# Two-layer decoder trunk, expert stage: slots in tiles of 64 and 32 instead of tiles of 32, down products of 512 columns

## The reference, cut to what matters

```python
D_MODEL = 1024; SEQ = 256; N_EXPERTS = 8; TOP_K = 2; D_FF_EXPERT = 3584
...
logits = (ht @ w_router).astype(jnp.float32) + b_router.astype(jnp.float32)
top_val, top_idx = lax.top_k(logits, TOP_K)
gates = jax.nn.softmax(top_val, axis=-1)
combine = jnp.sum(jax.nn.one_hot(top_idx, N_EXPERTS, dtype=jnp.float32) * gates[..., None], axis=1)
y = jnp.zeros_like(ht)
for e in range(N_EXPERTS):
    y = y + combine[:, e:e + 1].astype(h.dtype) * swiglu(ht, w_gate[e], w_up[e], w_down[e])
```

## Time and profile before

| | us |
|---|---|
| median of 3 runs | 1287.14 (1286.01 to 1287.77) |
| the profiled execution's own time | 1287.23 |
| its span, first to last instruction | 1285.4 |
| first product of the expert stage | at 464.13 |
| pairs 1, 2, 3 begin | at 663.80, 861.77, 1068.67 |
| last product of the small down of pair 3 ends | at 1274.93 |

### The profile page before, as it was taken

How to read it: one execution, slowest core, us unless ns; L and a number is a source line. 1 busy time by engine, 2 the same in 40 slices (tenths; PEclk the granted TensorE clock), 3 DMA queues, 4 the chain that set the end, 5 groups by cost and what they waited for, 6 DMA issues and landing times.

```text
span 1285.4 us, 27220 instructions
## 1 busy us (share of the span) xinstructions
PE 1233.9 (96%) x12500; PEld 712.8 (55%) x12501; DVE 338.3 (26%) x701; ACT 285.9 (22%) x499; POOL 39.3 (3%) x48
## 2 busy tenths in 40 slices
PE   7988999999999999999999999999997999998896
PEld 6865788888856763334653344653342664333364
DVE  5787565445357440000010010010020000001001
ACT  5575563434248411010000010000000000000000
POOL 1012000000003100000000000000000000000000
PEclk9999999999998999999999999999999999999999
DMA  9642455464453589999999999999999999999994
GB/s 352 233 131 97 134 177 185 129 236 160 113 178 132 222 369 412 412 415 425 424 424 425 427 425 425 424 424 426 425 427 426 425 424 424 425 427 426 425 423 170
DMA packets 64108, 423.64 MB, mean 330 GB/s; under 512 B 5760, under 2 KB 13686, under 8 KB 39414
## 3 DMA queue, kind: packets, MB, share of 16 engines
q1 hardware_dynamic: 62780, 419.09, 80.9%
q0 software_dynamic: 992, 2.69, 0.7%
q10 hardware_dynamic: 218, 0.08, 0.0%
HBM read 420.77 MB, written 1.07 MB: 328 GB/s over the span
## 4 chain that ended last, share of the span: by engine, by line
PE 81%; DMA 10%; DVE 4%; ACT 3%; issue 1%; SPq 0%; DVEq 0%; ACTq 0%
PE PS L2311 33%; PE PS L2340 16%; PE PS L1733 7%; PE PS L1737 7%; PE PS L1734 7%; DMA places_raw<-in_w_down_o_dram 6%; DMA places<-in_w_down_o_dram 3%; PE PS L2076 2%; PE PS L2348 2%; PE PS L2250 1%; DVE w_r L947 1%; PE PS L2233 1%; ACT w_r L487 1%; PE PS L2088 1%; DMA raw<-in_w_in_e_dram 0%
## 5 line engine op out<-in xcount | busy, mean ns | idle before, releaser
L2311 PE MATMUL PS<-places_raw,xe 128*32 128x512 f32 (+1 forms) x3760 | 362.4, 540 | 10.8 <-DMA places_raw<-in_w_up_o_dram 10.8
L2311 PEld LDWEIGHTS PS<-places_raw,xe 128*32 128x32 f32 x3760 | 119.4, 110 | 240.8 <-issue 218.8
L1733 PE MATMUL PS<-w_r,a_hi 128*128 128x512 f32 (+4 forms) x400 | 148.1, 374 | 3.5 <-DVE a_lo L976 2.5
L1734 PE MATMUL PS<-w_r,a_lo 128*128 128x512 f32 (+4 forms) x400 | 145.5, 367 | 0.0
L947 DVE TENSOR_TENSOR w_r<-raw,w_r 128x2048 fp32r<-128x2048 f32 (+4 forms) x61 | 128.9, 2142 | 42.0 <-ACT w_r L487 41.8
L2311 PE MATMUL PS<-places,xe 128*32 128x512 f32 (+1 forms) x1360 | 133.3, 540 | 4.1 <-DMA places<-in_w_up_o_dram 4.1
L487 ACT ACTIVATE w_r<-raw 128x2048 fp32r<-128x2048 f32 (+4 forms) x61 | 106.4, 1800 | 15.0 <-PE PS L1737 13.1
L2340 PE MATMUL PS<-places_raw,e_l 128*32 128x256 f32 x1848 | 106.4, 380 | 2.1 <-DMA places_raw<-in_w_down_o_dram 2.1
L1737 PE MATMUL PS<-w_r,a_hi 128*128 128x512 f32 (+4 forms) x400 | 103.7, 367 | 0.3 <-DVE w_r L947 0.3
L2311 PEld LDWEIGHTS PS<-places,xe 128*32 128x32 f32 x1360 | 43.3, 110 | 87.8 <-issue 80.2
L1733 PEld LDWEIGHTS PS<-w_r,a_hi 128*128 128x128 f32 x400 | 76.3, 191 | 17.4 <-issue 5.1
(11 more groups left out here) (328 smaller groups left out, 1011.6 us busy)
## 6 DMA issues: line engine op xcount, KB each, us to landing
places_raw<-in_w_gate_o_dram SPq DMA_DIRECT2D x48, 1792.0 KB, 27.0
places_raw<-in_w_up_o_dram SPq DMA_DIRECT2D x46, 1792.0 KB, 31.6
places_raw<-in_w_down_o_dram SPq DMA_DIRECT2D x44, 1792.0 KB, 37.2
places<-in_w_down_o_dram SPq DMA_DIRECT2D x19, 1792.0 KB, 36.5
places<-in_w_up_o_dram SPq DMA_DIRECT2D x18, 1792.0 KB, 32.5
places<-in_w_gate_o_dram SPq DMA_DIRECT2D x16, 1792.0 KB, 30.7
raw<-in_w_in_e_dram SPq DMA_DIRECT2D x12, 1024.0 KB, 9.8
raw<-in_w_down_e_dram SPq DMA_DIRECT2D x11, 1024.0 KB, 5.1
```

The lines of the kernel that those rows point to most:

```text
L1733: nc.tensor.matmul(dst, xh, wh, start=first, stop=False)
L1734: nc.tensor.matmul(dst, xl, wh, start=False, stop=False)
L2311: ins = nc.tensor.matmul(PS[g * Q:(g + 1) * Q, bank + c0 // NT, 0:c], xe[:, at, x0:x0 + Q], w[:, g * QW + c0:g * QW + c0 + c], start=at == ...
```

## The change

Tiles of the gate and up products: the first 64 slots are one block, loaded into two groups of 64 array columns. Pass `j` = 0 streams weight quarters 0 and 2, pass `j` = 1 quarters 1 and 3. The last 32 slots of a large expert stay a tile of 32 on four groups. Down: per block `kk` two matmuls of 512 columns for the 64 slots (each on one group of 64), and for a large expert four of 256 columns on groups of 32 as before. The results and the way back follow: `y_l` is [64 slots in two halves of the outputs] plus the tail's quarters, `y_s` one tile of 512 columns copied by ACT alone (DVE's `small_result` is gone), three pick matrices a pair instead of five, and `bring_back` contracts over 64 rows and, for the tail, over 32. Quarters are brought back and added in the order 0, 2, 1, 3.

```diff
+HALF_TILE = P // 2
+L_BLOCKS, BLOCKS = 2, 3
+BACK_ORDER = (0, 2, 1, 3)
...
-        LARGE_GATE, LARGE_UP, LARGE_DOWN = (2, 4, 0), (6, 2, 4), (0, 1, 6)
-        SMALL_GATE, SMALL_UP, SMALL_DOWN = (0, 6), (2, 4), (7, 5)
+        LARGE_GATE, LARGE_UP, LARGE_DOWN = (2, 4, 0), (6, 2, 4), (0, 1)
+        SMALL_GATE, SMALL_UP, SMALL_DOWN = (0, 6), (2, 4), 7
...
-        PICKS = ((2, 0), (2, S), (3, 0), (4, 0), (4, S))
+        PICKS = ((2, 0), (2, S), (4, 0))
...
-                for j in range(L_TILES):
-                    nc.scalar.activation(y_l[:, j, :], PS[:, LARGE_DOWN[j], 0:YC], ACT.Copy).then_inc(sem("l_y"), 1)
+                nc.scalar.activation(y_l[:, 0:NT], PS[:, LARGE_DOWN[0], :], ACT.Copy).then_inc(sem("l_y"), 1)
+                nc.scalar.activation(y_l[:, NT:NT + YC], PS[:, LARGE_DOWN[1], 0:YC], ACT.Copy).then_inc(sem("l_y"), 1)
...
-                nc.scalar.activation(y_s[:, 0, :], PS[:, SMALL_DOWN[0], 0:YC], ACT.Copy).then_inc(sem("s_y0"), 1)
+                nc.scalar.activation(y_s[:, :], PS[:, SMALL_DOWN, :], ACT.Copy).then_inc(sem("s_y"), 1)
...
             def return_picks(p):
 
+                if p:
+                    dve.wait_ge(mm_done, C_MOE + p * PAIR_CHUNKS)
...
-            def small_result(p):
-                dve.wait_ge(mm_done, C_MOE + (p + 1) * PAIR_CHUNKS)
-                nc.vector.tensor_copy(y_s[:, 1, :], PS[:, SMALL_DOWN[1], 0:YC]).then_inc(sem("s_y1"), 1)
...
-            def bring_back(of, y, tiles, banks):
+            def bring_back(of, y, tail_of, tail_y, banks):
 
                 for t in range(TT):
-                    for j in range(tiles):
-                        for g in range(4):
-                            rows_g = slice(g * Q, (g + 1) * Q)
-                            ins = nc.tensor.matmul(PS[:, banks[g], t * YC:(t + 1) * YC], of[rows_g, j, t * P:(t + 1) * P],
-                                                   y[rows_g, j, :], start=j == 0, stop=j == tiles - 1)
-                            if t == TT - 1 and j == tiles - 1:
-                                ins.then_inc(sem("moe_sc"), 1)
+                    rows_t, out = slice(t * P, (t + 1) * P), slice(t * YC, (t + 1) * YC)
+                    for g in BACK_ORDER:
+                        rows_c = slice(g // 2 * HALF_TILE, (g // 2 + 1) * HALF_TILE)
+                        ins = nc.tensor.matmul(PS[:, banks[g], out], of[rows_c, rows_t], y[rows_c, g % 2 * YC:(g % 2 + 1) * YC],
+                                               start=True, stop=tail_y is None)
+                        if tail_y is None and t == TT - 1:
+                            ins.then_inc(sem("moe_sc"), 1)
+                    for g in BACK_ORDER if tail_y is not None else ():
+                        rows_g = slice(g * Q, (g + 1) * Q)
+                        ins = nc.tensor.matmul(PS[:, banks[g], out], tail_of[rows_g, rows_t], tail_y[rows_g, :],
+                                               start=False, stop=True)
+                        if t == TT - 1:
+                            ins.then_inc(sem("moe_sc"), 1)
...
-                x0 = (L_CAP if small else 0) + j * Q
                 bank = {"g": (LARGE_GATE, SMALL_GATE), "u": (LARGE_UP, SMALL_UP)}[kind][small][j]
+                if j < 2:
+                    x0, n, of = (L_CAP if small else 0), HALF_TILE, lambda g: (2 * g + j) * QW
+                else:
+                    x0, n, of = HALF_TILE, Q, lambda g: g * QW
                 for c0, c in ((0, NT), (NT, QW - NT)):
-                    for g in range(4):
-                        ins = nc.tensor.matmul(PS[g * Q:(g + 1) * Q, bank + c0 // NT, 0:c], xe[:, at, x0:x0 + Q],
-                                               w[:, g * QW + c0:g * QW + c0 + c], start=at == 0, stop=at == DC - 1)
+                    for g in range(P // n):
+                        ins = nc.tensor.matmul(PS[g * n:(g + 1) * n, bank + c0 // NT, 0:c], xe[:, at, x0:x0 + n],
+                                               w[:, of(g) + c0:of(g) + c0 + c], start=at == 0, stop=at == DC - 1)
...
-                    for j in range(S_TILES if small else L_TILES):
-                        bank = (SMALL_DOWN if small else LARGE_DOWN)[j]
+                    first, last = G == 0 and kk == 0, G == 3 and kk == QB - 1
+                    at = kk * P + G // 2 * HALF_TILE
+                    for c in range(2):
+                        ins = nc.tensor.matmul(PS[c * HALF_TILE:(c + 1) * HALF_TILE, SMALL_DOWN if small else LARGE_DOWN[0], :],
+                                               acts[:, G % 2, at:at + HALF_TILE], down_columns(n - half, kk, c * NT, NT),
+                                               start=first, stop=last)
+                    if not small:
+                        at = kk * P + G * Q
                         for g in range(4):
-                            ins = nc.tensor.matmul(PS[g * Q:(g + 1) * Q, bank, 0:YC],
-                                                   acts[:, j, kk * P + G * Q:kk * P + (G + 1) * Q], down_columns(n - half, kk, g),
-                                                   start=G == 0 and kk == 0, stop=G == 3 and kk == QB - 1)
+                            ins = nc.tensor.matmul(PS[g * Q:(g + 1) * Q, LARGE_DOWN[1], 0:YC], acts[:, 2, at:at + Q],
+                                                   down_columns(n - half, kk, g * YC, YC), start=first, stop=last)
```

More of the change, by code:

```diff
@@ L225, in hybrid_trunk @@
         e_l, z = place(z0, "e_l", [P, L_TILES, QW])
[L226 removed]
+        y_l, _ = place(z0, "y_l", [P, NT + YC])
         rt, _ = place(z0, "rt", [P, 9, TT * NE * NE])
[L228 to L229 removed]
+        y_s, _ = place(z, "y_s", [P, NT])
+        gpick, _ = place(z + NT, "gpick", [P, TT, BLOCKS, P])
         e_s, z = place(z, "e_s", [P, S_TILES, QW])
[L231 removed]
+        back_s, z = place(z, "back_s", [P, S])
+        z += S
         places, z2 = place(z, "places", [P, 3, EW])
@@ L464, in _ @@
                 sp.wait_ge(sem("spare_add"), 4 * SPARES)
-            for g in range(4):
+            for n, g in enumerate(BACK_ORDER):
                 cols = slice(g * YC, (g + 1) * YC)
-                sp.wait_ge(sem("moe_add"), 8 * PAIRS - 3 + g)
+                sp.wait_ge(sem("moe_add"), 8 * PAIRS - 3 + n)
                 sp.dma_start(out[0].rearrange("(t p) d -> p t d", p=P)[:, :, cols], X[:, :, cols]).then_inc(sem("stored"), 16)
@@ L1544, in return_picks @@
             def return_picks(p):
+                if p:
+                    dve.wait_ge(mm_done, C_MOE + p * PAIR_CHUNKS)
                 for t in range(TT):
[L1547 to L1550, removed]
+                    for j, (e, s0, n) in enumerate(((p, 0, HALF_TILE), (p, HALF_TILE, Q), (p + PAIRS, 0, HALF_TILE))):
+                        ins = nc.vector.tensor_scalar(gpick[:, t, j, :].rearrange("p (a s) -> p a s", s=n),
+                                                      iota[:, s0:s0 + n].unsqueeze(1).to_broadcast([P, P // n, n]),
                                                       pos[:, t, e:e + 1], comb[:, t, e:e + 1], ALU.is_equal, ALU.mult)
@@ L1608, in pair @@
                     gathered(p + 1)
-                for g in range(4):
+                for g in BACK_ORDER:
                     add_back(2 * p, g, BACK_L[g])
-                small_result(p)
                 if not follow:
-                    for g in range(4):
+                    for g in BACK_ORDER:
                         add_back(2 * p + 1, g, LAST_BACK[g])
@@ L2242, in turn_picks @@
                 ins.then_inc(sem("moe_turn"), 1)
[L2244 removed]
+            def bring_back(of, y, tail_of, tail_y, banks):
                 for t in range(TT):
[L2247 to L2253 removed]
+                    rows_t, out = slice(t * P, (t + 1) * P), slice(t * YC, (t + 1) * YC)
+                    for g in BACK_ORDER:
+                        rows_c = slice(g // 2 * HALF_TILE, (g // 2 + 1) * HALF_TILE)
[9 more added lines that the diff above has]
+                            ins.then_inc(sem("moe_sc"), 1)
             def back_large(p):
[L2257 to L2258 removed]
+                pe.wait_ge(sem("l_y"), L_BLOCKS * (p + 1))
+                bring_back(back_l[:, 0, :], y_l[:, 0:NT], back_l[:, 1, :], y_l[:, NT:NT + YC], BACK_L)
             def back_small(p, banks):
[L2262 to L2264 removed]
+                pe.wait_ge(sem("s_y"), p + 1)
+                bring_back(back_s, y_s, None, None, banks)
             def two_rows(block, f):
@@ L2277, in tile_waits @@
                 elif k == 0 and j == 1:
-                    if p:
-                        pe.wait_ge(sem("s_y1"), p)
-                    else:
+                    if not p:
                         pe.wait_ge(sem("x_dve"), 1)
@@ L2319, in gate_up, with down_columns @@
                 ins.then_inc(mm_done, 1)
-            def down_columns(n, kk, g):
-                if kk < 3 or (kk == 3 and g < 2):
-                    return place_of(n)[:, kk * D + g * YC:kk * D + (g + 1) * YC]
-                return place_of(n + 1)[:, kk * D + g * YC - EW:kk * D + (g + 1) * YC - EW]
```

(4 more changed lines are left out.)

14 lines of the change are left out of this document (6 added, 8 removed).

## The result

| | before | changed |
|---|---|---|
| median us | 1286.88 (1286.01 to 1287.77, 4 runs) | 1312.48 (1312.23 to 1315.52, 4 runs) |
| ratio | 1 | 1.0205, 95% interval 1.0188 to 1.0221 |
| profiled execution: own time, span | 1287.23, 1285.4 | 1315.52, 1313.7 |
| expert stage, first product to last | 464.13 to 1274.93, 810.8 | 465.98 to 1303.27, 837.3 |

The changed kernel is 2% slower, 25.6 us in the medians. The forecast was 1313.5. One of the ten executions of the first grouped kernel further down ran at a granted clock of 0.75 and took 1601.42 us, and its ratio leaves it out.

A forecast was written before the change was run, and what follows sets the result against it. The transfers bound the kernel, PE having 21.7 us in hand. PE's end, 1253.2 + 47.4 + 0.7 = 1301.3, passes the transfers' 1274.9; with the tail's -0.2 that is +26.2, so 1313.5 us, range 1300 to 1322.

The forecast's parts named there:

- The bound: Expert stage: the transfers bound the old kernel, and PE has 21.7 us in hand.
- Streamed columns, side by side: Large gate, up and down products: no streaming saved, two 64-wide groups run side by side, 0.435 us for two rounds.
- Rival D: Gate, up and down: groups of 64 don't overlap for 512 columns, some 1840 us; chance 1%.
- Fewer instructions: nothing: PE's matmuls: no overhead in an instruction that a wider one could save, so no gain.
- Rival E: Whole kernel: it gets faster; only the tail's -0.2 us is left, PE can't pull the transfers; chance 2%.
- Changes of width: Large-expert chunks: 340 changes between 64 and 32 columns, 0.16 or 0.12 us each, add 47.4 us on PE.
- small terms: PE: way back +1.7 us, 64-wide after 128-wide work +0.9, fewer pick transposes -1.9; sum +0.7.
- The tail: After the last product: single ACT copy +0.2 us, earlier adds on DVE -0.4, together -0.2.
- The slack as a rule: PE in the expert stage: added work is free up to 21.7 us and counts in full beyond.
- Rival A: Expert stage: the change of width costs nothing or under 0.06 us, transfers still bound, 1287 us; chance 11%.
- B: Width changes: only the leaving costs, 0.10 us each, 1300 us, the low end; with forecast and C 86%.
- C: Each width change costs half a way to 128 and back, 1322 us, the high end; with forecast and B 86%.

The follow-up runs named there:

- grouped kernel: The changed kernel with 64-wide and 32-wide products reordered to stand together, 96 changes of width instead of 340: 1284.27 us, repeated with more rounds 1282.78 us.
- half loads: From the twelfth chunk on only half of each chunk is loaded, PE's work unchanged: kernel before 1266.98 us, changed kernel 1313.84 us.
- kernels with 18 us more: The kernel before with 18.1 us of 32-wide tile passes repeated: over all four pairs 1294.59 us, in pairs 2 and 3 alone 1290.39 us.
- split one: The grouped kernel with every gate and up matmul of 512 or 384 columns split into two of half the columns: 1287.26 us, ratio 1.0001.

## Why the prediction was right

*The bound.* Right. PE had some 21 us to wait out in the old kernel (half loads: 21.1 below the kernel before of the same runs, worked out 21.7), none in the new one.

*Streamed columns, side by side.* Right: a 64-wide round of 512 takes 0.43 us for both groups; the rounds start 0.43 us apart, 0.48 right after a change of width. Rival D is gone.

*Fewer instructions: nothing.* Right for PE's time and wrong for the kernel as a whole. The step costed only what an instruction costs on TensorE. What the number of instructions does to the transfers, by their fetches as it seems, was left out, and where the transfers are the bound it is worth some 4 us. In the changed kernel, which PE bounds, it is hidden. Rival E rested on the same gap: "PE can't pull the transfers" is so, but with fewer instructions the last weights land earlier, and the grouped kernel is 0.2 to 0.3% faster than the one before.

*Changes of width.* The step that carries the sum. 340 changes at 0.12 and 0.16 gave 47.4 us; with the small terms 48.1 for the stage's four pairs, 12.0 each. Pair 1 grew by 12.03. The stage grew by 26.5 us (worked out 26.4). So the number came out right because its parts did, each within 1 us, and not by luck: the slack was 21.1 us by the half loads (worked out 21.7), and the added work 46.9 (worked out 47.9). That neighbours' prices can be composed, the leaving by one and the first load by the other, held to 0.01 us. The 64-wide half of a block holds its first load and the leaving of 64, 0.05 + 0.10 by the prediction's prices and 1.01 - 0.86 = 0.15 in the chain; the 32-wide half 0.02 + 0.11, and 0.57 - 0.435 = 0.135 in the chain. The rule of the Trainium skill (TensorEngine Tiling (Array Packing), Key Properties), that a change of tiling mode drains TensorE, agrees with this trace for 64 against 32, where the way there and back costs 0.28 us; the page has no figure.

*The tail.* -0.2 worked out, -0.26 measured.

*Against the median.* The profiled execution of the changed kernel lies 3.0 us above the median of its four. Its stage begins 1.85 us later than in the kernel before, in code that was not changed: over the 84 to 86 us ahead of the stage the mean granted clock is 0.92 here and 0.94 there, which is 1.8 us. From profile to profile the difference is 28.3 us, 26.5 of it in the stage; the medians differ by 25.6.

*The slack as a rule.* "Work added is free up to 21.7 us" was too simple, and the kernels with 18 us more show it: spread over all pairs they lengthen the span by 7.0 us, in pairs 2 and 3 alone by 1.9. In pair 0 PE holds the transfers. It did no harm here, since the added work was far beyond the slack. For a change that adds 10 to 20 us it would have given the wrong answer.

*Rival A* (no cost), *B* (only the leaving, 0.10) and *C* (0.165) lie outside what was measured, 0.14 to 0.15.

## What to carry to other kernels

Tiles of different width on one array are cheap only if each width runs in long stretches: here a change between 64 and 32 columns costs 0.14 to 0.15 us, about a third of a round of 512 columns, and grouping them took 28 to 30 us off the changed kernel and left it 0.2 to 0.3% below the old one. When an engine and the transfers both look full, work out from a stretch without waits what the engine alone would need; the difference is what it may lose, but not in the stretch where the ring is short of places. And where the DMA engines are the bound, ask what the number of instructions does to them: here it was worth 4 us.

## What the runs showed of the hardware

- The shares of one transfer drift apart: from chunk 17 to chunk 191 (750 us) the fastest of the 16 gains 14 us on the slowest in the kernel before, 7.4 in the grouped one, eight shares keep together ahead and eight behind, and the slowest decides when a chunk has landed.
- Instruction fetches are 16 KB packets of about 1.06 us among the DMA queues. Against the grouped kernel's 61 the kernel before has 99 and takes 4.3 us longer, the split one 85 and 4.5 us longer; that the fetches are the cause is argued.
- Not all device time lies between a program's first and last instruction: 1.8 to 1.9 us are outside in most kernels here, 3.1 to 3.8 in two of them, in each of their executions.
- The price of leaving a width hardly depends on whether the next is wider or narrower (32 for 64 0.11, 32 for 128 0.12, 64 for 32 0.10, 64 for 128 0.10, 128 for 32 or 64 0.09), and the first weight load grows with the width, 0.02 for 32, 0.05 for 64, 0.10 for 128 columns.
